# Layer 1's convolution one column to the right, and layer 1 one tile behind the channel mixer

## What is computed

```python
for l in range(2):
    h = rmsnorm(x, norm1_g[l])
    z = h @ w_in[l]                                  # u | v | lru_x | lru_gate | gate_A | gate_B
    y_a = gelu(u) * mix128(layernorm(gelu(v)))       # 128 x 128 matrix per group, per 128 positions
    xc = conv_b + sum(pad(zx, 1, 2)[:, k:k + S] * conv_w[k] for k in range(4))
    r, i = sigmoid(blockdiag(xc, w_r)), sigmoid(blockdiag(xc, w_i))
    a = exp(-8 * r * softplus(-lam)); b = sqrt(1 - a * a) * i * xc
    hrec = scan_forward(a, b) + scan_backward(a, b)  # h_t = a_t h_(t-1) + b_t, each direction its weights
    y_b = hrec * gelu(zg)
    x = x + (sigmoid(gate_A) * y_a + sigmoid(gate_B) * y_b) @ w_out[l]
    g, u = split(rmsnorm(x, norm2_g[l]) @ w_ffn_in[l])
    x = x + (silu(g) * u) @ w_ffn_out[l]
return rmsnorm(x, final_g)
```

## Time and profile before

| | us |
|---|---|
| median of 3 runs | 4154.54 (4151.74 to 4713.47) |
| profiled execution | 4158.18 |
| span of its slowest core (core 0) | 4156.6 |
| spans of the eight cores | 4099.3 to 4156.6 |
| TensorE busy on core 0 | 3690.1 |

### The profile page before, as it was taken

One profiled execution on the slowest core, in us unless ns is written; L12 is line 12 of the kernel. 1 busy time (PEld: TensorE's weight loads), 2 busy tenths in 40 slices (PEclk: granted clock), 3 DMA queues, 4 the chain that ended last, 5 costly groups with the idle time before them and its releaser, 6 DMA issues.

```text
span 4156.6 us, 55798 instructions; the slowest of 8 cores (4099.3 to 4156.6 us)
## 1 busy us (share of the span) xinstructions
PE 3690.1 (89%) x17522; PEld 1694.5 (41%) x17874; DVE 2242.3 (54%) x3267; ACT 2529.8 (61%) x3494; POOL 349.0 (8%) x595
## 2 busy tenths in 40 slices
PE   4777777698998989999999999867999999999988
PEld 2333333243444444444444444433444444444443
DVE  4677777744365564656566462765364444444422
ACT  5677788763648576675858672886384645735211
POOL 2111111010100010000000000000000000000000
PEclk9899899899999999999999999997999999999999
DMA  9668877789987979697887665774666676674643
GB/s 197 128 127 149 149 167 173 223 173 260 180 260 203 247 206 236 227 236 244 219 259 217 209 211 174 227 232 143 206 230 219 199 238 198 212 247 154 207 161 106
DMA packets 354911, 836.90 MB, mean 201 GB/s; under 512 B 35184, under 2 KB 159296, under 8 KB 340416
## 3 DMA queue, kind: packets, MB, share of 16 engines
q1 hardware_dynamic: 238880, 767.24, 58.4%
q0 software_dynamic: 115744, 66.07, 14.1%
HBM read 748.27 MB, written 206.57 MB: 230 GB/s over the span
## 4 chain that ended last, share of the span: by engine, by line
PE 72%; DMA 8%; ACT 8%; issue 6%; DVE 3%; POOL 1%; SPq 0%; ACTq 0%; DVEq 0%; POOLq 0%
PE pfall L1153 28%; PE pfall L975 15%; PE pfall L1172 14%; PE pfall L959 4%; PE pfall L1129 3%; DMA YA<-guth 3%; PE pfall L702 2%; PE pfall L929 2%; PE pfall L1208 2%; DMA xm<-XC 2%; PE pfall L616 1%; DMA hf<-HF 1%; DMA xr<-XL 1%; DMA xs<-x 1%; ACT ra L718 1%
## 5 line engine op out<-in xcount | busy, mean ns | idle before, releaser
L1153 PE MATMUL pfall<-hTa,wr 128*128 128x512 bf16 x2753 | 627.1, 383 | 36.0 <-ACT sg L1158 20.1
L1153 PE MATMUL pfall<-hTb,wr 128*128 128x512 bf16 x2759 | 618.8, 381 | 8.6 <-ACT hTb L1143 3.5
L1172 PE MATMUL pfall<-wr,ff 128*128 128x512 bf16 x2759 | 607.6, 379 | 3.9 <-ACT sg3b L1158 0.9
L975 PE MATMUL pfall<-hTa,wr 128*128 128x512 bf16 x1868 | 428.4, 381 | 16.3 <-ACT guth L977 9.5
L1153 PEld LDWEIGHTS pfall<-hTa,wr 128*128 128x128 bf16 x2816 | 276.6, 99 | 368.1 <-issue 49.1
L1153 PEld LDWEIGHTS pfall<-hTb,wr 128*128 128x128 bf16 x2816 | 276.6, 98 | 342.0 <-issue 14.0
L1172 PEld LDWEIGHTS pfall<-wr,ff 128*128 128x128 bf16 x2816 | 275.4, 98 | 333.5 <-issue 1.4
L1129 PE MATMUL pfall<-wr,mT 128*128 128x512 bf16 x1007 | 237.7, 392 | 65.5 <-DVE mT L1118 46.9
L886 DVE SCALAR_TENSOR_TENSOR xm<-zb,cols,xm 128x512 f32<-128x512 f32 x384 | 277.5, 746 | 33.3 <-ACT hz L936 13.3
L1177 DVE TENSOR_TENSOR xr<-pfall,xr 128x512 f32<-128x512 f32 x128 | 80.3, 684 | 386.6 <-PE pfall L1172 386.0
L975 PEld LDWEIGHTS pfall<-hTa,wr 128*128 128x128 bf16 x1920 | 186.5, 98 | 235.8 <-issue 21.0
(11 more groups left out here) (145 smaller groups left out, 5276.1 us busy)
## 6 DMA issues: line engine op xcount, KB each, us to landing
wr<-WB SPq DMA_DIRECT2D x832, 512.0 KB, 5.6
XC<-xm SPq DMA_DIRECT2D x32, 1024.0 KB, 9.7
YA<-guth SPq DMA_DIRECT2D x128, 256.0 KB, 5.3
HF<-ib SPq DMA_DIRECT2D x32, 1024.0 KB, 10.0
xm<-XC SPq DMA_DIRECT2D x32, 1024.0 KB, 7.8
ya<-YA SPq DMA_DIRECT2D x128, 256.0 KB, 6.9
hf<-HF SPq DMA_DIRECT2D x128, 256.0 KB, 6.7
WB<-w_ffn_in POOLq DMA_DIRECT2D x44, 512.0 KB, 21.1
```

Source lines behind the costliest of these rows:

```text
L975: op = sc.mm(key, p, [(lambda e, k=k: e.matmul(p.f(), lhsT=w(k), rhs=hT[:, k, lo:lo + TT], start=(k == 0), stop=(k == KC - 1)), bh + [bw]) ...
L1153: op = sc.mm(keyf(t), p, [(lambda e, k=k, o=o, q=q, p=p: e.matmul(p.f(), lhsT=q[:, k, o:o + 128], rhs=hT[:, k, 0:TT], start=(k == 0), stop ...
L1172: sc.mm(keyf(nb, q, s), ps[s], [(lambda e, f=f, s=s, t=t, q=q, p=ps[s]: e.matmul(p.f(), lhsT=fs[f][0][:, s * 128:(s + 1) * 128], rhs=t[:, ...
```

## The change

Layer 1's convolution and backward recurrence of tile j now cover positions 512 j + 1 to 512 j + 512, so that they need no column to the left. The halo of three columns comes from the tile to the right alone. Their results go to two new HBM tensors, XC1 and HB1, laid out along the whole sequence (a row of 2 KB for each partition and block), from which stage 3 reads tiles at their own positions. Position 0 of the sequence is left over: `first_column` computes its convolution, gates and recurrence on 128 x 8 elements at the end, and stores them as 1024 single elements each to XC1 and HB1. Layer 1 follows by one tile (ja = j + 1): passes 1 to 7 have both parts, pass 8 (tile 0) the layer-1 part alone, and pass 9 is gone. Layer 1's input has one buffer and not two. Pass 0 copies 16 weight chunks, not 12, and pass 1 copies 8, not 12. In stage 3 the gates R of tile 2 stand among the first channel mixer's FO matmuls and not behind them.

```diff
-    def zx1(c, j, key, keyh, wzx):
+    def zx1(c, j, key, wzx):
...
-        if j == NT - 1:
-            ph = P("t")
-            sc.mm(keyh, ph, [(lambda e, k=k: e.matmul(
-                ph.f(0, 2), lhsT=w(k), rhs=hT[:, k, TT:TT + 2], start=(k == 0), stop=(k == KC - 1)),
-                [bh[NS - 1], bw]) for k in range(KC)], 0.065)
-            sc.op("dve", lambda e: e.tensor_copy(out=z[:, c, 0:1], in_=ph.f(1, 2)), 0.2, writes=[bz[c]], psum=[ph])
         p = P("main")
         sc.mm(key, p, [(lambda e, k=k: e.matmul(
-            p.f(), lhsT=w(k), rhs=hT[:, k, 1:TT + 1], start=(k == 0), stop=(k == KC - 1)), bh + [bx, bw])
+            p.f(), lhsT=w(k), rhs=hT[:, k, :], start=(k == 0), stop=(k == KC - 1)), bh + [bw])
...
-            xcstore(j, XM8, c // 4)
+            xcstore1(j, XM8, c // 4)
+    def first_column(key):
...
+        sc.dma("sp", lambda e: e.dma_start(out=XC1[:, :, 0:1], in_=lone[:, 0:1, :].rearrange("p o c -> p c o"),
+                                                allow_slow_non_contiguous=True), 4096,
+               reads=[blone], writes=bXC1[0])
...
+        dv(lambda e: e.tensor_mul(out=v(7), in0=v(4), in1=ca), [bca])
+        dv(lambda e: e.tensor_add(out=v(7), in0=v(7), in1=v(6)))
+        sc.dma("sp", lambda e: e.dma_start(out=HB1[:, :, 0:1], in_=lone[:, 7:8, :].rearrange("p o c -> p c o"),
+                                                allow_slow_non_contiguous=True), 4096,
+               reads=[blone], writes=bHB1[0])
...
-        for s in (3, 0, 1, 2):
+        for s in range(NS):
...
-    T1AT = {1: 3, 3: 0, 5: 1, 6: 2}
-    ZAT = {3: [0], 4: [1], 5: [2], 6: [3, 4], 7: [5, 6, 7]}
+    T1AT = {1: 0, 2: 1, 3: 2, 4: 3}
+    ZAT = {4: [0], 5: [1, 2], 6: [3, 4], 7: [5, 6, 7]}
     xtp = None
-    for i in range(NT + 2):
+    for i in range(NT + 1):
         j = NT - 1 - i
         g = G2 + i
-        ja = j + 2 if j + 2 < NT else None
+        ja = j + 1 if j + 1 < NT else None
...
+            if j < 0:
+
+                a = [t for t in a if t[0] != "R1"]
+                for n, c in enumerate(range(KC)):
+                    a.insert(2 + n + n // 2, ("R1", c))
+                a.insert(20, ("LONE", 0))
...
-                cast_next(2 if i < 2 and f % 6 == 0 else 1, op)
+                cast_next(2 if i == 0 else 1, op)
...
         if j == 0:
-            tok += [("R", c) for c in range(KC)]
+            for c in range(KC):
+                tok.insert(tok.index(("FO", c // 6, c % 6, NS - 1)) + 1, ("R", c))
```

More of the change, by code:

```diff
@@ L487, in _build @@
     XL = scratch("XL", [NT, 128, NS, D], F32)
+    XC1 = scratch("XC1", [128, KC, S + 8], F32)
+    HB1 = scratch("HB1", [128, KC, S + 8], F32)
     sc = Sched(nc, stack)
@@ L563, in _build @@
     bYA = [[Buf("YA") for _ in range(KC)] for _ in range(NT)]
+    bXC1 = [[Buf("XC1") for _ in range(2)] for _ in range(NT + 1)]
+    bHB1 = [[Buf("HB1") for _ in range(2)] for _ in range(NT + 1)]
     bXL = [[Buf("XL") for _ in range(NS)] for _ in range(NT)]
@@ L888, in conv, with xcstore1, xcload1, hbstore @@
                     op0=ALU.mult, op1=ALU.add), 0.75, reads=[bzb, bcols, bxm], writes=[bxm])
+    def xcstore1(j, xm, h):
+        t0 = j * TT + 1
+        sc.dma("sp", lambda e: e.dma_start(out=XC1[:, 4 * h:4 * h + 4, t0:t0 + TT], in_=xm.group(h)),
+               XHALF, reads=[xm[4 * h + i][1] for i in range(4)], writes=[bXC1[j + 1][h]])
+    def xcload1(j, xm, h):
+        sc.dma("sp", lambda e: e.dma_start(out=xm.group(h), in_=XC1[:, 4 * h:4 * h + 4, j * TT:(j + 1) * TT]),
+               XHALF, reads=[bXC1[j][h], bXC1[j + 1][h]], writes=[xm[4 * h + i][1] for i in range(4)])
+    def hbstore(j):
+        t0 = j * TT + 1
+        for h in range(2):
+            sc.dma("sp", lambda e, h=h: e.dma_start(out=HB1[:, 4 * h:4 * h + 4, t0:t0 + TT], in_=ib[:, 4 * h:4 * h + 4, :]),
+                   XHALF, reads=bib[4 * h:4 * h + 4], writes=[bHB1[j + 1][h]])
     def xcstore(j, xm, h):
@@ L1060, in stream @@
         no, n, cols, b = wchunks[l][name, i]
+        if not b.w:
+            raise RuntimeError(f"chunk {l} {name} {i} has not been copied")
         t, bt = wring.next()
@@ L1402, in mixer @@
     def mixer(c, j, key0, key1, gur, thr):
-        return merge(c, j, (key0, key1), hTa[0], 0, hTa[1], sgx.block(c), sgb.block(c), gur, thr)
+        return merge(1, c, j, (key0, key1), hTa[0], 0, hTa[1], sgx.block(c), sgb.block(c), gur, thr)
     hfr = TR("hf", 3, [128, TT], F32, HVA)
```

105 lines of the change are left out of this document (64 added, 41 removed).

## The result

The changed kernel takes 4747 us in the median of six runs (4617 to 5072), the kernel before 4261 in the same session, with 4152 as its fastest. Both medians hold executions in which the cores of one die ran longer at a lower granted clock; over the others the ratio is **1.119, with a 95% interval of 1.108 to 1.131**. The forecast was 4143 us and "within 2%". It was wrong: the fastest run is 11% above it.

What follows compares the result with a forecast made beforehand. TensorE was taken to bound most of the program, an engine-to-engine chain the end of stage 2. Terms summed to -11.5 us, 4146.7 against the profile's 4158.2; less 3.6 for the runs' median, 4143 us, range 4108 to 4176.

Steps and rivals of the forecast that it cites:

- Larger DMA patterns: XC1 and HB1 stored in 2 KB rows instead of 8 KB: no gain, at most somewhat later stores, 0.
- Pass 9 goes, -66: End of stage 2: a 71.3 us stretch leaves the chain, Z starts some 5 us later in pass 8; -66 us.
- second rival: End of stage 2 into stage 3: chain shortens by more than pass 9, up to 10 us; 4122 us, chance 0.18.
- Pass 1 +51.5: Pass 1 gains a layer-1 part: from 188.9 us to pass 3's 240.4, so +51.5 us.
- Pass 2 -6: Pass 2 loses the first-tile halo matmuls and their waits: 246.4 us towards pass 3's 240.4, so -6 us.
- Z behind T1 +11: Seven passes: Z waits for the copy of the transposes just ahead, 1.5 us each; +11 us (0 to 28).
- Gates R among FO and stage 3, -7: Stage 3: gates among FO save 9.7 us, the following OP of tile 2 loses 2.5; together -7 us.
- Position 0 +3: Start of stage 3: small store delays hf loads, first merges 7 us late, much taken up; +3 us (0 to +13).
- The third rival: Start of stage 3: small store takes 20 us, not 6, delaying hf and OP; 4154 us, chance 0.06.
- the forecast's two readings of 1024 descriptors: Single-element store: either its fixed time dominates and the term stays +3, or the skill's warning means a slow store.
- the casts' 2: Four more casts in pass 0, four fewer in pass 1: between 0 and +8 us, taken as +2.
- a tight merge stretch (4171): Between first G and OP, VectorE falls behind and OP waits: 4 us in each of seven passes, +28; chance 0.22.

Runs made afterwards that it cites:

- the first three experiments: Changed kernel with stores at column 512 j: 1.029; that with pitch 16,896 B: 0.996; changed kernel with stores at 512 j + 128, pitch 17,408 B: 0.998.
- the crossed cell: Changed kernel with the pitch of XC1 and HB1 rows 16,896 B instead of 16,416 B, stores still at column 512 j + 1: 0.997 (0.993 to 1.001).

## Why the prediction was wrong

**The step that failed** is "Larger DMA patterns ... No gain, and at most a store that lands some us later, for loads that come passes later: 0". It argued from hf loads, which move 2-KB rows, to stores. The direction was wrong (loads from the new layout are fast, stores slow), and the number at issue was not the rows' size at all but their pitch, which the text didn't weigh. The term of 0 measured +476 us: 4617.3 against 4141.5, the fastest runs of the changed kernel and of the one with the pitch of 16,896 B and nothing else changed (in two sessions, whose fastest runs of the kernel before differ by 4 us). That pair is the whole error. The step looked only at who loads the stored data, passes later. It didn't ask who may not overwrite ib until the store has landed, nor what else the same DMA engines move meanwhile.

**The rest of the sum** can be read from the run with the pitch of 16,896 B, the same change without the slow stores. Its windows: pass 1, 2, 3, passes 4 to 7, pass 8, stage 3's start, the rest:

```profile
970.20:1236.82 266.62, 235.41 (x1105) 106.57 (x1104) 136.96 (x199) 160.72 (x219) 18.51 (x32) 0.94 0.85 217
1236.82:1477.66 240.84, 226.79 (x1106) 104.63 (x1104) 137.49 (x199) 161.21 (x219) 19.30 (x32) 0.99 0.84 229
1477.66:1718.55 240.89, 228.29 (x1105) 104.97 (x1104) 137.72 (x199) 161.39 (x219) 19.43 (x32) 0.98 0.85 229
1718.55:2661.80 943.25, 902.12 (x4401) 416.68 (x4399) 529.41 (x767) 597.85 (x820) 66.06 (x117) 0.99 0.77 223
2661.80:2752.83 91.03, 68.89 (x352) 31.94 (x353) 61.28 (x100) 77.11 (x113) 8.25 (x16) 0.90 0.82 248
2752.83:2859.90 107.07, 66.09 (x258) 26.66 (x257) 62.27 (x90) 71.84 (x104) 3.83 (x8) 0.74 0.53 167
2859.90:4146.10 1286.20, 1245.97 (x5888) 568.44 (x5888) 549.74 (x741) 617.72 (x809) 69.94 (x120) 0.99 0.61 199
```

- *Pass 9 goes, -66*: from the last FO to stage 3's channel mixer 198.1 us, before 265.0: **-66.9**, with the column of position 0 inside. The sum is right and its parts are not: pass 8 is 91.0 us for 77.3, +13.7 where the forecast had +5, and stage 3's start 107.1 for 116.4, -9.3, which is the second rival's gain. That they cancel is luck. All four T1 took from 2665.0 to Z at 2675.1, 10.1 us, where the forecast had 11.3.
- *Pass 1 +51.5*: 266.6 for 188.9, **+77.7**, so 26 too little. TensorE waits there 10.37 us for the copy of hz, 5.4 for mT in two waits and 5.6 for a Silu. That copy stands behind a cast on ScalarE that waits 11.3 us for VectorE's convolution, and VectorE, in its turn, waits 12.3 and 4.2 us for hf loads, as the timeline shows. Against pass 3, 18.6 of the 25.7 us more are idle time of TensorE, and 7.1 are the same matmuls at a clock of 0.94 for 0.98. The pass with DMA share 0.90 before is where I should have asked which load comes late.

```profile
999.61 0.69 DVE L1140 TENSOR_TENSOR hf<-hf,ib 128x512 f32<-128x512 f32 x1 [12.29 <-DMA hf<-HF]
...
1006.50 0.69 DVE L1140 TENSOR_TENSOR hf<-hf,ib 128x512 f32<-128x512 f32 x1 [4.20 <-DMA hf<-HF]
```

- *Pass 2 -6*: 240.8 for 246.4, **-5.6**.
- *Z behind T1 +11*: eight waits, 11.8 us in all, 1.5 each, as said. But passes 3 to 7 together are 1184.1 us for 1182.4, **+1.7**: most of it is taken up later in the pass. The low end was the truer one.
- *Gates R among FO and stage 3, -7*: 1286.2 for 1299.0, **-12.8**. OP stands straight behind FO, took 17.3 us and waited 3.13 for xr, as said (18.3 and 3.0). The forecast called the clock of OP of tile 1 before low; over 3013.94:3029.75 it was 0.87.
- *Position 0 +3*: with the pitch of 16,896 B the second single-element store landed after 4.6 us, the estimate was 6. In the changed kernel it took 24.5, and the first one held VectorE for 41.5. The rival's sign came too: VectorE waited 23.5 us for an hf load at stage 3's start. The third rival had the right mechanism and the wrong cause: not small pieces, but small pieces at that pitch. At the other pitches the same store landed after 3.3 to 5.7 us, so of the forecast's two readings of 1024 descriptors the runs bear out the cheap one there.
- Ahead of pass 1 the run gained 4.7 us. Altogether 4146.1 against 4156.6, **-10.5** where the sum had -11.5. Pass 1 came out 26 us too long, and that was balanced by the passes after it (9 less), stage 3 (6), the start (7, with the casts' 2) and the end (4); the agreement is luck to that extent, and it is between two single executions, of kernels whose runs spread over more than that.

The rivals: a tight merge stretch (4171) did not come. Its sign, OP waiting for mT, did show in the changed kernel (89.3 us in 17 waits), but with the pitch of 16,896 B that is 36.2 us in 8 waits, before 46.9 in 13; so it came from the slow stores. The shorter chain came within stage 3's start and not beyond the sum. No rival had a price for a store, and 0.02 for slower by over 2% was far too sure of a layout that no row of the profile had shown. The bound that I set myself, from both sides by the nearest row, was taken from a load; with ib's single buffer and a DMA share of 0.83 to 0.90 in a pass, it needed a store's row, and the earlier trace rows has none. "No wait of TensorE in stage 2 is released by a DMA" was true and looked one step too short: over 850:2860 of the kernel before, ScalarE waits 34.6 us for xm's loads and 9.5 for YA's stores, and VectorE 14.6 for hf loads.

With other pitches and its results unchanged, the changed kernel lies between 0.997 and 1.003 of the kernel before; 16,896 B has 0.997 (0.993 to 1.001). The 10 us of the two profiles are within that, so the runs don't tell the worth of the change from nothing.

## What to carry to other kernels

A new layout in HBM is a change of its own: measure its stores alone, with the pitch and the start that it will have, before arguing about the order of work; a store of 1 MB that takes 20 us and not 6 shows at once. Of the first three experiments two changed pitch and start at a time, and all three agreed with the wrong theory; only the crossed cell (new pitch, old start) told them apart. Compare a landing time with that of the like transfer in the same stage: stage 1's 4.9 us was no measure for stage 2. When the same bytes and the same packets take more DMA time, look for the transfer whose landing has grown, and then for whoever may not overwrite its source.
